# Sample attention with keys transposed in 32x32 blocks on VectorE and scored in sixteen 32x32 tiles of TensorE

## What is computed

```python
s = einsum('bthr,bsr->bhts', ql, ckv) + einsum('bthp,bsp->bhts', qp, kpe)
s = where(k_pos <= q_pos, s * ATTN_SCALE, -inf)
p = softmax(s, axis=-1)
o = einsum('bhts,bsr->bthr', p, ckv)      # the latent keys are the values too
```

## Time and profile before

| | |
|---|---|
| time, median of 3 runs | 2452.96 us (2446.86 to 2453.09) |
| time of the profiled execution | 2453.16 us, its span 2451.3 us |
| TensorE busy | 2155.4 us, 88% of the span |
| VectorE, ScalarE, GpSimd busy | 1003.5, 460.7, 337.6 us |
| mean granted TensorE clock | 0.951 of full speed |
| sample stage, first transpose to last score | 1572.1 to 1751.7 us of the span |

### The profile page before, as it was taken

How to read it: one execution, slowest core, us unless ns; L and a number is a source line. 1 busy time by engine, 2 the same in 40 slices (tenths; PEclk the granted TensorE clock), 3 DMA queues, 4 the chain that set the end, 5 groups by cost and what they waited for, 6 DMA issues and landing times. The chain is left out here.

```text
span 2451.3 us, 52576 instructions
## 1 busy us (share of the span) xinstructions
PE 2155.4 (88%) x21060; PEld 1375.3 (56%) x21061; DVE 1003.5 (41%) x1904; ACT 460.7 (19%) x918; POOL 337.6 (14%) x458
## 2 busy tenths in 40 slices
PE   5999999849999998799678999799999399899987
PEld 3666654436666664466445555566544276576653
DVE  1334233342222223459887555454333522222226
ACT  1323211100000001242223555333211000000001
POOL 0000000012222222056400000001000022122112
PEclk9999999969999999899898999899999699999999
DMA  6111233257868745611202000255151548764847
GB/s 212 38 34 35 85 123 111 95 186 274 328 257 311 301 158 187 202 36 42 81 20 103 6 6 0 99 218 194 59 195 52 223 168 311 297 229 172 348 171 283
DMA packets 148587, 382.85 MB, mean 156 GB/s; under 512 B 11592, under 2 KB 71128, under 8 KB 146472
## 3 DMA queue, kind: packets, MB, share of 16 engines
q1 hardware_dynamic: 110160, 276.62, 30.4%
q0 software_dynamic: 16480, 82.77, 9.2%
q10 hardware_dynamic: 21880, 22.55, 2.8%
HBM read 336.89 MB, written 45.00 MB: 156 GB/s over the span
## 5 line engine op out<-in xcount | busy, mean ns | idle before, releaser
L302 PE MATMUL PS<-xT,W 128*128 128x352 f32 x960 | 286.6, 461 | 28.7 <-ACTq L311 28.7
L497 PE MATMUL PS<-wo,yT 128*128 128x512 f32 x576 | 261.9, 604 | 0.6 <-issue 0.6
L302 PEld LDWEIGHTS PS<-xT,W 128*128 128x128 f32 x960 | 183.2, 191 | 130.4 <-ACTq L311 28.3
L786 PE MATMUL PS<-xT,yst 128*32 128x256 f32 x3648 | 212.9, 385 | 29.7 <-DVE yst L857 19.1
L1020 PE MATMUL PS<-xT,W 128*128 128x352 f32 (+1 forms) x672 | 204.0, 467 | 34.5 <-ACT qT L1095 21.8
L797 PE MATMUL PS<-w,yst 128*32 128x256 f32 x3360 | 203.6, 379 | 14.6 <-DVE yst L872 14.1
L857 DVE STREAM_TRANSPOSE yst<-yst 128x256 f32<-128x256 f32 x150 | 66.8, 445 | 353.1 <-PE PS L786 334.4
L832 ACT ACTIVATE yst<-PS 128x128 f32<-128x128 f32 x150 | 41.7, 278 | 808.4 <-PE PS L786 670.7
L786 PEld LDWEIGHTS PS<-xT,yst 128*32 128x32 f32 x3648 | 142.2, 111 | 90.9 <-issue 40.6
L1020 PEld LDWEIGHTS PS<-xT,W 128*128 128x128 f32 (+1 forms) x672 | 127.3, 190 | 110.9 <-issue 46.9
L786 PE MATMUL PS<-yT,yst 128*32 128x256 f32 x3072 | 176.3, 379 | 11.8 <-issue 11.8
(11 more groups left out here) (349 smaller groups left out, 2528.2 us busy)
## 6 DMA issues: line engine op xcount, KB each, us to landing
xT<-in_w_exp_in SPq DMA_DIRECT2D x24, 2048.0 KB, 14.6
w<-in_w_exp_out SPq DMA_DIRECT2D x22, 2048.0 KB, 13.6
yT<-in_w_exp_in SPq DMA_DIRECT2D x20, 2048.0 KB
wo<-in_w_exp_in SPq DMA_DIRECT2D x20, 2048.0 KB, 13.8
xrn<-in_w_exp_out SPq DMA_DIRECT2D x10, 2048.0 KB, 14.3
yb<-yst ACTq DMA_DIRECT2D x150, 128.0 KB
W<-in_w_in_even SPq DMA_DIRECT2D x20, 512.0 KB, 3.9
xm<-xrn SPq DMA_DIRECT2D x18, 512.0 KB, 2.9
```

The source lines that it names most:

```text
L302: ins = nc.tensor.matmul(PS[:, n % 5, 0:CW], W5[:, p, k, :], xT[:, k, c * CW:(c + 1) * CW], start=(k == 0), stop=(k == KD - 1))
L497: ins = nc.tensor.matmul(PS[:, mix_bank(t) + n, :], yT[:, k, t * P:(t + 1) * P], wo[:, k, n * 512:(n + 1) * 512], start=(first and k == ks ...
L786: ins = nc.tensor.matmul(PS[q * GR:(q + 1) * GR, 0, 0:2 * P], xtb[:, k, :], w1[s][:, k, q * 2 * P:(q + 1) * 2 * P], start=(k == 0), stop=( ...
```

## The change

The keys are no longer transposed by TensorE. VectorE transposes each half in 32x32 blocks, SBUF to SBUF, by four STREAM_TRANSPOSE of 128 x 1024 and one of 128 x 512 (`turn_keys`). A block transpose leaves each 32-row strip of positions in its own 32 partitions, with 32 channels across them, so `scores` now works in 32x32 tiles: for each of 9 chunks of 32 channels (8 latent, 1 rotary), each of 4 strips of partitions and each of 4 groups of slots, one product of 32 rows by 32 queries by 128 columns. That is 144 products per half in place of 24. The strips write to PSUM banks 0 to 3. Queries must stand in all four strips: eight products with the 0/1 matrix `fold` replicate them once for all sequences (`qlr`), and the rotary queries are copied to four strips (`qpr`, 32 copies as before, without the zero fill). The scores against the new tokens are formed once for all sequences, ahead of the bodies. ScalarE copies the transposed weights in place of VectorE. `KL[1]` lies in `wo[:, 0:4]`, so half of the output weights is loaded after the last score; `wukT` goes to `wo[:, 6:8]` and is loaded during the prompt stage.

```diff
 def sp_prompt(sp):
-            load_wo(sp, 1)
+            sp.dma_start(wo[:, 4:6, :], wout[:, 4:6, :]).then_inc(sem("in_wo"), 16)
+            sp.dma_start(wukT, io["wukT"]).then_inc(sem("in_uk"), 16)
 def sp_sample(sp):
             sp.wait_ge(sem("a_qns"), 8)
+            sp.wait_ge(sem("d_ql"), 1)
+            sp.dma_start(wo[:, 6:8, :], wout[:, 6:8, :]).then_inc(sem("in_wo"), 16)
+            sp.wait_ge(sem("d_s"), 2 * SEQS)
             for n in range(2):
-                sp.dma_start(wukT[n], io["wukT"][:, 4 * n:4 * n + 4, :]).then_inc(sem("in_attn_w"), 16)
+                sp.dma_start(wo[:, 2 * n:2 * n + 2, :], wout[:, 2 * n:2 * n + 2, :]).then_inc(sem("in_wo1"), 16)
 def pe_sample(pe):
+            for r in range(2):
+                for c in range(4):
+                    ins = nc.tensor.matmul(PS[:, c, r * 256:(r + 1) * 256], fold[QS * c:QS * (c + 1), :],
+                                           qlat[QS * c:QS * (c + 1), r, :, :].rearrange("p b q -> p (b q)"), start=True, stop=True)
                 def scores(h):
-                    for r in range(2):
-                        for g in range(4):
-                            nc.tensor.matmul(PS[g * QS:(g + 1) * QS, 4, :], qb[:, s, r, :], CT[g][:, r, :], start=(r == 0), stop=False)
-                    for j in range(4):
-                        for g in range(4):
-                            ins = nc.tensor.matmul(PS[g * QS:(g + 1) * QS, 4, j * P:(j + 1) * P], qpb[:, s, j, :], KT[:, g, :], ...)
+                    pe.wait_ge(sem("d_kt"), b * 2 + h + 1)
+                    for c in range(KD + 1):
+                        for rows in range(4):
+                            strip = slice(rows * QS, (rows + 1) * QS)
+                            turned = KL[h][strip, :].rearrange("p (n d) -> p n d", d=KV_RANK)[:, :, c * QS:(c + 1) * QS] if c < KD else \
+                                KR[strip, h, :].rearrange("p (n d) -> p n d", d=ROPE)
+                            for g in range(4):
+                                ins = nc.tensor.matmul(PS[g * QS:(g + 1) * QS, rows, 0:P], qb[strip, s, c, :], turned[:, 4 * g:4 * g + 4, :],
+                                                       start=(c == 0), stop=(c == KD))
...
-                turn(0, 0, 0), turn(0, 1, 1), turn_rotary(0, 2), turn(0, 2, 3), turn(0, 3, 4), and the same for half 1
...
             sequences(pe, body)
-            mix_piece(0, 1, [5, 6, 7], False, True).then_inc(sem("m_mm"), 1)
+            pe.wait_ge(sem("in_wo1"), 32)
+            for n in range(2):
+                ins = mix_piece(0, n, [0, 1, 2, 3], False, True)
 def act_sample(act, A):
-                ins = AC(CT[...]/KT, PS[...], ACT.Copy)      # ten times per sequence
+                def take_weights(h, n):
+                    AC(PTd[:, h, :, :].rearrange("p a b -> p (a b)"), PS[:, 4, :], ACT.Copy).then_inc(sem("d_pt"), 1)
 def dve_sample(dve, D):
+            def turn_keys(b, s, h, p):
+                cols = slice(1024 * p, 1024 * (p + 1))
+                nc.vector.transpose(KL[h][:, cols], half_of(s, h)[:, cols])
+                if p == 3:
+                    nc.vector.transpose(KR[:, h, :], half_of(s, h)[:, SLOTS * KV_RANK:SLOTS * ROW]).then_inc(sem("d_kt"), 1)
             def body(b, s, first, last):
-                take(0), take(1), take_weights(1), take(3), take(4), maximum(0), take(5), take(6), take_weights(0), take(8), take(9)
+                turn(0,0), turn(0,1), maximum(1 of b-1), turn(0,2), turn(0,3), turn(1,0), turn(1,1), maximum(0), turn(1,2), turn(1,3)
```

More of the change, by code:

```diff
@@ new lines, in pe_sample @@
+            ins.then_inc(sem("d_qr"), 1)
+            pe.wait_ge(sem("d_qp"), 1)
+            for b in range(SEQS):
+                new_keys = PS[0:QS, 5, b * SAMPLE:(b + 1) * SAMPLE]
+                for r in range(2):
+                    nc.tensor.matmul(new_keys, qlat[:, r, b, :], ckvT[:, r, PROMPT:TOK], start=(r == 0), stop=False)
+                ins = nc.tensor.matmul(new_keys, qpr[0:ROPE, b, :], kpeS[:, :], start=False, stop=True)
+            ins.then_inc(sem("d_qr"), 1)
+            pe.wait_ge(sem("d_qp"), 3)
@@ L1488, in body, with scores @@
+            pe.wait_ge(sem("d_qa"), 3)
+            pe.wait_ge(sem("a_yt"), 2 + 32)
             def body(b, s, first, last):
[L1490 to L1494, removed]
+                def scores(h):
+                    pe.wait_ge(sem("d_kt"), b * 2 + h + 1)
+                    if not (first and h == 0):
+                        pe.wait_ge(sem("d_e"), b * 2 + h)
@@ L1495, in free @@
                     part(pe)
[L1497 to L1505, removed]
@@ L1521, in turn_weights, with weigh @@
                     ins.then_inc(sem("d_p"), 1)
-                def scores(h):
-                    pe.wait_ge(sem("d_cta"), b * 10 + 5 * h + 5)
-                    pe.wait_ge(sem("d_ctd"), b * 10 + 5 * h + 5)
-                    for r in range(2):
-                        for g in range(4):
-                            nc.tensor.matmul(PS[g * QS:(g + 1) * QS, 4, :], qb[:, s, r, :], CT[g][:, r, :], start=(r == 0), stop=False)
-                    for j in range(4):
[L1531 to L1538, removed]
+                def weigh(sv, h, n):
+                    pe.wait_ge(sem("d_pt"), n + 1)
                     for j in range(4):
@@ L1562, in body @@
                     nc.tensor.transpose(PS[0:1, 5, 0:P], mxr[:, :], ident)
[L1563 removed]
+                    turn_weights(1, b * 2 - 1)
                 if last:
[L1565 to L1568, removed]
+                    pe.wait_ge(sem("in_wo"), 64)
+                    pe.wait_ge(sem("a_yt"), 2 + 32)
+                    pe.wait_ge(sem("m_ps"), 9 + 1)
+                    mix_piece(0, 0, ks[4:6], True, False)
                 if not first:
+                    weigh(1 - s, 1, b * 2 - 1)
                     pe.wait_ge(sem("d_mr"), b)
@@ L1600, in body @@
                 if not last:
-                    for r in range(2):
-                        nc.tensor.matmul(PS[0:QS, 5, A_SN:A_SN + SAMPLE], qb[:, s, r, :], ckvT[:, r, PROMPT:TOK], start=(r == 0), stop=False)
-                    nc.tensor.matmul(PS[0:QS, 5, A_SN:A_SN + SAMPLE], qpb[0:ROPE, s, 0, :], kpeS[:, :], start=False, stop=True)
                     scores(1)
@@ L1654, in body @@
                 if not last:
-                    take(5)
                     expo(s, 0, b * 2)
-                    for k in range(6, 10):
-                        take(k)
+                    take_weights(0, b * 2)
                 if not first:
@@ L1709, in maximum @@
                     TS(nmh[:, sv, h:h + 1], mx, -SCALE, None, ALU.mult).then_inc(sem("d_nm"), 1)
+                if not last and not first:
+                    turn(0, 0)
+                    turn(0, 1)
                 if not first:
@@ L1730, in body @@
                 if not last:
+                    turn(1, 0)
+                    turn(1, 1)
                     maximum(b, s, 0, b * 2)
-                    take(5)
                 if not first:
@@ L1745, in body @@
                     D(TS(wr2[:, :], wh[:, :], rdd[:, :], None, ALU.mult))
-                if not last:
-                    take(9)
-                if not first:
                     dve.wait_ge(sem("d_pv"), b * 2)
@@ L1751, in body @@
                     mul_add(olr[:, :], out_bank(1 - s, 1), wr2[:, 1:2], olr[:, :]).then_inc(sem("d_ol"), 1)
+                if not last:
+                    turn(1, 3)
             with D.rounds(0, 1, 1):
                 body(0, 0, True, False)
-            with dve.Fori(0, 3) as i, D.rounds(i, 2 * 12, 3):
+            with dve.Fori(0, 3) as i, D.rounds(i, 2 * 10, 3):
                 body(i * 2 + 1, 1, False, False)
```

164 lines of the change are left out of this document (67 added, 97 removed).

## The result

The change makes the kernel slower: 2546.89 us (2543.73 to 2553.79, 4 runs) against 2453.03 us, ratio 1.039 (95% interval 1.036 to 1.042). The forecast was 2424 us, range 2410 to 2497.

A forecast was written before the change was run, and what follows sets the result against it. TensorE was taken as the bound, 22.8 us a sequence, falling to 18.5. 2453.2 - 11.2 (start) - 30.1 (seven periods) - 2.2 (last body) + 3.7 (tail) + 2 (instruction supply) + 8 (clock) gave 2424 us, range 2410 to 2497.

The forecast's parts named there:

- S: Time of the new score products of one half on TensorE: 2.2 us taken, up to 8.9 for the range.
- the term for instruction supply: Fetching TensorE's longer loop body, about ten packets a pass, mostly beside work: +2 us, bounds 0 and +10.
- S's cover: Two VectorE transposes between a half's last transpose and the maximum of its scores hide 2.5 us of S.
- the first rival: Every score instruction, loads too, takes a 7.5 ns slot: S = 4.3, T = 22.1, 2447 us; chance 0.20.
- The same burst: In the experts of the earlier trace, 4 MATMUL and 8 LDWEIGHTS begin within 0.09 us, 7.5 ns an instruction.
- The second rival: 32x32 score products start no faster than 128x32 ones, 27.3 ns: S = 7.9, T = 29.3, 2502 us; chance 0.27.
- T: Period of one sequence in the sample stage: 18.5 us, longer where S exceeds 2.5, against 22.8 before.
- Two falls: TensorE's granted clock drops twice in gaps behind score blocks, about 4 us each: +8 us, bounds 0 and +32.
- The rival of falls in every sequence: The granted clock falls in every sequence: +32 us in place of +8, 2448 us; chance 0.03.
- VectorE's period: VectorE's time for one sequence: transposes 11.4, other work 4.2, between instructions 1.3, waits 1.55, together 18.5 us.
- the start: Start of the sample stage: weights loaded early, so first scores come at about 1568, 11.2 us earlier.
- the tail: After the last score, projection pieces wait for output weights loaded late; about 7.3 us of pieces move: +3.7 us.

The follow-up runs named there:

- e4: Changed kernel with the score products of chunks 1 to 7 run as a loop, always on chunk 1, so fewer instructions are fetched: 2488.33 us.
- e15: Changed kernel with 16 wide score products a half in place of 144 (not the reference's scores) and two filler products behind each half's scores: 2425.30 us.
- e10: e4 with two filler products behind each half's scores to keep TensorE busy: 2449.40 us.
- e9: Changed kernel with two filler products of 512 columns behind each half's scores, to keep the clock up: 2544.28 us.
- e13: Changed kernel with chunk 1 looped in place of chunks 1 to 7 in half 0 only, half 1 written out: 2516.5 us.
- e16: Changed kernel with chunk 1 looped five times in place of chunks 1 to 5 in both halves, the others written out: 2488.5 us.
- e7: e4 with every score product 16 columns wide in place of 128: 2483.46 us.
- e1: Changed kernel with 16 products a half on all 128 rows in place of 144 small ones (not the reference's scores): 2443.78 us.

## Why the prediction was wrong

**The step that failed** is S, and with it the term for instruction supply. The prediction took 2.2 us for the scores of a half, from sixteen tiles that overlap, and +2 us for fetching; measured were 8.9 us. The 576 instructions alone need 4.7 (e4), and the rest is waiting for them to be fetched, which made the largest single loss, +59 us.

**The ladder.** Runs that differ by one cause each, from the forecast to the result: e15 2425 (S 2.4, clock mostly full, program kept), e10 2449 (S 4.8), e4 2488 (clock falls), changed kernel 2547 (program fetched, S 8.9). So +24 for the slots of the instructions, +39 for the clock, +59 for instruction supply. From the first to the last scores, which leaves out what differs ahead of the stage, the four take 147.7, 177.1, 211.8 and 268.7 us: +29, +35, +57. By e9 the last two aren't independent: where the fetching sets the pace, the clock costs little or nothing more.

**Instruction supply: the term was mis-sized, and this is the largest part.** The prediction took +2 us, bounds 0 and +10. The mechanism was named, and that some ten packets a pass would come was right (14 in 91 us, with passes of 72). Wrong was the price. I used the duration of a packet, 1.1 us, and concluded that 2.25 packets would just fit in S's cover of 2.5 us; what counts is the distance between packets, 3.2 us at best in the changed kernel, and longer behind a gather, which was in flight in most of the scores. The runs show this by what removes it: without the 384 further instructions a half (e4) no wait for "issue" is left. With them, 576 instructions in a row run faster than they are delivered. The row that should have warned stands in the prediction itself: instructions 7.5 ns apart mean a block of 256 in 1.9 us.

The Trainium skill, "Runtime: NRT & Kernel Launch", section "Instruction fetch mechanics", says that blocks of 256 instructions, 16 KiB, are fetched while the one before is executed; the size agrees (14 packets, 0.23 MB). Its room for 2048 instructions on TensorE doesn't agree with e13, where a body of 1,900 was fetched in every pass, nor with the third pass of e16 (1,650). It also says that issue is slow enough to hide the fetching; at 7.4 ns an instruction that doesn't hold (27.7 us of "issue" in 138 us).

**S: the wrong end was taken.** The lower bound, 2.2 us from all sixteen tiles overlapping, was called the likeliest; e7 shows the first rival's slots, 576 x 7.4 = 4.3, and e4 4.7 with full columns. The same burst of the earlier trace rows carried both numbers, and the one that counts loads should have been taken, since the burst begins an instruction of either kind every 7.5 ns. The second rival's 27.3 ns and its 2502 us came nearest to the result, but not its mechanism: a MATMUL with its load takes 15 to 16 ns. So the 25 ns of "TensorE: Matmul & The Clock Gate", section "Wait — 56ns, not 53.3ns?", in the Trainium skill don't hold between different 32x32 tiles here. That rival also called TensorE the bound again at T = 29.3 us, where its own sum gives TensorE 7.2 + 15.8 = 23 us of work; what it really priced is the chain through VectorE.

**The clock: mis-sized.** Two falls, +8 us, were taken; in e4 the mean granted clock is 0.75 from the third period on, and against e10 it costs some 4.3 us of a period of 27.3. Even with S = 2.4 it falls in every sequence: e1's seven periods take 152.5 us, where seven at the full clock would take an estimated 125 (17.9 each, from e15, which even has more work), so falls cost at least 27 us. The rival of falls in every sequence, 3 in 100, was right in what happens, and its +32 is of the size of these 27 and of the 39 us between e4 and e10.

**Right:** VectorE's period (18.5 forecast, 17.8 in e15) and its transposes, though its parts were off both ways: VectorE is busy 14.9 us and not 15.6, waits 2.4 and not 1.55, and 0.5 are left between instructions and not 1.3; the cover, T = 18.5 + 2 x (S - 2.5), gives 23.1 at e10's S of 4.8 (measured 22.7 to 23.8); the start, 12.6 us forecast from entry to first scores (the changed kernel 15.5, at half clock in part); the tail, +3.7 forecast, +5.5 measured. With S = 8.9 that formula gives 31.3 of the mean 35.4 us seen. The other 4 us aren't fully explained: in the changed kernel the two products with the values run at half clock, 1.4 to 1.7 us longer each, but e9 has the same period with the clock mostly up.

## What to carry to other kernels

Count instructions, not only columns: at 7.4 ns each, loads included, 576 of them need 4.3 us whatever they compute, and a float32 product brings four. Here a long stretch that used a block of 256 in 1.9 us waited for its program, since the blocks came 3.1 us apart at best and later under large gathers; a loop body on TensorE of about 1,400 instructions was exempt. And when work leaves an engine that was busy all the time, ask what the gaps do to its clock before counting them as free.

## What was not expected of the hardware

Packets of instructions that last 1 us start no closer than 3.1 us apart, but for three pairs in e13 and e16. A body of 1,650 instructions is kept through most of the second pass and fetched again in the third, one of 1,390 not at all. Sixteen-tile products of 16 and of 128 columns differ by only 0.4 us in 288 MATMULs (4.3 against 4.7). At half the granted clock the slots of the instructions keep their 7.4 ns (e7 at 0.50: 4.23 us), while 128 columns go from 4.7 to 5.8 us.
